# The dilated stage's first norm kept as one number per token, its row spread inside the second weight group

## The chip, the cores and the metric

The kernel runs on one core of one Trainium2 chip. The metric is the device time of one execution in microseconds (us); the median of several executions counts. TensorE (PE) multiplies matrices, VectorE (DVE) and ScalarE (ACT) work element by element, GpSimd (POOL) makes the low halves of the weights, and SyncE (SP) issues the weight transfers.

## The reference

Two transformer blocks follow one another on 512 tokens of width 1024. The second layer of the second block is the dilated attention. Its keys and values come from a norm of their own of the residual stream `x`:

```
def rmsnorm(x, g):
    xf = x.astype(jnp.float32)
    y = xf * lax.rsqrt(jnp.mean(xf * xf, axis=-1, keepdims=True) + RMS_EPS)
    return (y * g).astype(x.dtype)
...
    kv = (rmsnorm(x, kv_norm) @ w_kv).reshape(B, S, 2, N_GROUPS, ATT_HEADS, ATT_HEAD_DIM)
...
    h = rmsnorm(x, norm_mix_pre[layer])
    m = dilated_mixer(h, att_w_q[bi], att_w_o[bi], k_sh, v_sh, pos)
```

Both norms are of the same `x`, so they share one number per token, the reciprocal root of the mean square. It is this number, for all 512 tokens, that the change makes in another way.

## The kernel before

Everything is held with features on the 128 partitions and tokens along the row. `x` is eight tiles of 128 features by 512 tokens. A product of full precision is three matmuls of 512 columns (lines 702, 703 and 704: high by high, low by high, high by low); one such triple of one 128 by 128 weight tile is a k-step, and eight k-steps fill a bank. The gain of the norm is put into the operand (`h_hi` by ACT, `h_lo` by DVE), the reciprocal root is multiplied in later, when a bank is taken out (evicted).

The order on each engine is that of the code, with semaphores between engines. The start of the dilated stage (the function `dilated` of each engine) runs so:

1. The postnorm of the stage before updates `x` tile by tile. As each tile is ready ACT makes its high halves and its squares `SQD` (`dil_sq` in the trace), DVE the low halves.
2. PE runs the **first group**: three banks together, eight k-steps each, with the operands `H2H`, `H2L`.
3. PE adds up the squares with eight products of the 128 by 128 matrix of ones (the stationary operand) by `SQD[:, k, :]` (512 columns), line 1156. The result is a whole bank: on every partition the sum of each of 512 tokens. Each product shows in the trace as two matmuls.
4. PE runs the **second group**: two banks together, eight k-steps each, with `HH`, `HL` (`h_hi`, `h_lo`), each k waiting for its `h_lo` of line 2206. Four more banks follow singly.
5. DVE meanwhile: the fourth `h_lo`, then (`variance`, line 1613) mean and epsilon over 128x512; ACT takes the root of 128x512 (`std`, line 1206); DVE makes the fifth `h_lo`, then the reciprocal over 128x512 (`inverse`, line 1619) into `RSTD`, then the last three `h_lo`. It multiplies `RSTD` into the cosines and sines (line 2301), and evicts nine banks in the order `DIL_FIRST_OUT = (4, 0, 1, 2, 6, 3, 5, 7, 8)`. The first to be evicted is the second bank of the second group, and it waits until that group is done.
6. The first scores (`s_pair`, line 1053) wait until the rotary sums of six of these banks are done (`rotated`, line 2230).

Elsewhere in the kernel the same norm is made in columns: `column_sums` (line 733) takes 128 tokens of the squares as the stationary operand and one column of ones as the moving one, four products for 512 tokens, each again two matmuls in the trace; `spread` (line 742) turns a column of 128x4 numbers back into a row on all partitions by four transposes.

Of the kernel before, what the change touches and what calls it, by code (L numbers as in the profile page):

```python
# [20 lines left out]
ALU = mybir.AluOpType  # L21
ACT = mybir.ActivationFunctionType
# [4 lines left out]
D = 1024  # L27
KT = D // P
# [9 lines left out]
EPS = 1e-6  # L38
# [4 lines left out]
S0, TURN, OUTB = 3, 5, 7  # L43
# [97 lines left out]
DIL_FIRST_BANKS = (0, 1, 3, 4, 5, 6, 0, 1, 0)  # L141
# [142 lines left out]
def by_class(x):  # L284

    return x.rearrange("p (j r) -> p r j", r=4)


def in_class(x):

    return x.rearrange("p (r j) -> p r j", r=4)
# [12 lines left out]
def two_stacks_kernel(nc, d, out):  # L304
# [3 lines left out]
    with ExitStack() as ctx:  # L308
        sems = {n: ctx.enter_context(nc.semaphore(n)) for n in SEMAPHORES}

        def sb(name, shape, dt=F32):
            return ctx.enter_context(nc.sbuf_tensor(name, shape, dt))

        X = sb("x_res", [P, KT, SEQ])
        HH = sb("h_hi", [P, KT, SEQ], F32R)
        HL = sb("h_lo", [P, KT, SEQ], F32R)
# [6 lines left out]
        ONES = sb("ones", [P, P])  # L323
        RSTD = sb("rstd", [P, SEQ])
        RSTD2 = sb("rstd2", [P, SEQ])
        VAR = sb("var", [P, SEQ])
# [8 lines left out]
        def at(name, shape, offset, dt=F32):  # L335
            size = int(np.prod(shape[1:])) * 4
            assert offset + size <= arena_bytes, (name, offset + size, arena_bytes)
            return nc.alloc_sbuf_tensor_at(name, shape, dt, offset=base + offset)
# [82 lines left out]
        SQD = at("dil_sq", [P, KT, SEQ], 33 * T1)  # L421
# [12 lines left out]
        def sm(c, n=1):  # L434
            return SM[:, c:c + n]

        def gain(name, k=0):
            c = GAINS[name] + k
            return G[:, c:c + 1]

        banks = [ctx.enter_context(nc.psum_tensor(f"bank{b}", [P, SEQ], F32)) for b in range(8)]
# [201 lines left out]
        def _(pe):  # L643
            t = Tally(pe)

            class Programs:
                mine, stage = "stage_pe", 0
                n, tiles, rot, steps, gates = 0, 0, 0, 0, 0
# [60 lines left out]
                    for k in range(KT):  # L709
                        self.kt(bank, hi, lo, k, k == 0, k == KT - 1)  # L710

                def together(self, opened, hi, lo, nk, fresh, spread=None):

                    for k in range(nk):
                        if k == 1 and spread is not None:
                            self.spread(spread)
                        if k >= nk - fresh:
                            pe.wait_ge(sems["operand"], t.at("operand", k + 1 - nk))
                        elif k == 0:
                            pe.wait_ge(sems["operand"], t.at("operand", -fresh))  # L720
                        for bank in opened:
                            self.kt(bank, hi, lo, k, k == 0, k == nk - 1)
# [22 lines left out]
                def mix(self, l):  # L745
# [88 lines left out]
                    def turn(n, i):  # L834
                        _, blocks = key_blocks(KINDS[n], i)
                        if t.k.get("pt_copied", 0):
                            pe.wait_ge(sems["pt_copied"], t.at("pt_copied", CREDITS["pt_copied"]))
                        if i == 0:
                            pe.wait_ge(sems["v_token"], t.at("v_token"))
                        for m in range(group(KINDS[n])):  # L840
                            t.up("probs")
                            pe.wait_ge(sems["probs"], t.at("probs"))
                            for b in range(blocks):
                                ins = pe.transpose(banks[TURN + m][:, b * P:(b + 1) * P], SS[i % 2][m][:, b * P:(b + 1) * P], ID[:])  # L844
                            ins.then_inc(sems["turned"], t.one("turned"))
                            t.up("pt_copied")
# [178 lines left out]
                def dilated(self):  # L1025
# [125 lines left out]
                    opened = [self.open(b) for b in DIL_FIRST_BANKS[0:3]]  # L1151
                    self.together(opened, H2H, H2L, KT, KT)
                    for k in range(KT):
                        t.up("dil_squared")
                        pe.wait_ge(sems["dil_squared"], t.at("dil_squared"))
                        ins = pe.matmul(banks[OUTB][:], ONES[:], SQD[:, k, :], start=(k == 0), stop=(k == KT - 1))
                    ins.then_inc(sems["summed"], t.one("summed"))
                    t.up("operand", KT)
                    self.together([self.open(b) for b in DIL_FIRST_BANKS[3:5]], HH, HL, KT, KT)
                    base = self.tiles - 5  # L1160
                    out = {x: base + DIL_FIRST_OUT.index(at_) for at_, x in enumerate(DIL_FIRST)}
                    for at_ in range(5):
# [1 line left out]
                    for at_, x in list(enumerate(DIL_FIRST))[5:]:  # L1164
                        bank = self.open(DIL_FIRST_BANKS[at_])
# [18 lines left out]
        def _(act):  # L1184
            t = Tally(act)
# [12 lines left out]
            def root():  # L1198
                t.up("var_ready")
                act.wait_ge(sems["var_ready"], t.at("var_ready"))  # L1200
                act.activation(sm(INV, QT), sm(INV, QT), ACT.Sqrt).then_inc(sems["std_ready"], t.one("std_ready"))

            def std():
                t.up("var_ready")
                act.wait_ge(sems["var_ready"], t.at("var_ready"))
                act.activation(VAR[:], VAR[:], ACT.Sqrt).then_inc(sems["std_ready"], t.one("std_ready"))

            class Programs:
                mine, stage = "stage_act", 0
                n, tiles = 0, 0  # L1210
# [281 lines left out]
                def dilated(self):  # L1492
# [75 lines left out]
                            act.activation(in_class(HH[:, j, :]), by_class(X[:, j, :]), ACT.Copy, scale=gain("kv", j)).then_inc(sems["kv_hi"], t.one("kv_hi"))  # L1568
                    t.up("cleared", 6)
                    self.past(3, KT)  # L1570
                    std()
                    self.past(2, KT)
                    self.past(1, KT)
                    self.v_out(DVT[0][:, 0], DAUX)
# [16 lines left out]
        def _(dve):  # L1591
            t = Tally(dve)
# [13 lines left out]
                dve.tensor_tensor(lo, src, hi.bitcast(F32), ALU.subtract).then_inc(sems[name], t.one(name))  # L1606
                dve.wait_ge(sems[name], t.at(name))

            def variance(bank, n, placed=lambda x: x, taken=lambda x: x):

                t.up("summed")
                dve.wait_ge(sems["summed"], t.at("summed"))
                dve.tensor_scalar(placed(VAR[:]), taken(banks[bank][:]), 1.0 / n, EPS, ALU.mult, ALU.add).then_inc(sems["var_ready"], t.one("var_ready"))

            def inverse(dst=RSTD):

                t.up("std_ready")
                dve.wait_ge(sems["std_ready"], t.at("std_ready"))
                dve.reciprocal(dst[:], VAR[:]).then_inc(sems["dve_step"], t.one("dve_step"))
                dve.wait_ge(sems["dve_step"], t.at("dve_step"))  # L1620

            def rstd(bank, n, dst=RSTD):

                variance(bank, n)
                inverse(dst)

            def inverses(bank, n):

                t.up("summed")
                dve.wait_ge(sems["summed"], t.at("summed"))  # L1630
                dve.tensor_scalar(sm(INV, QT), banks[bank][:, 0:QT], 1.0 / n, EPS, ALU.mult, ALU.add).then_inc(sems["var_ready"], t.one("var_ready"))
                t.up("std_ready")
                dve.wait_ge(sems["std_ready"], t.at("std_ready"))
                dve.reciprocal(sm(INV, QT), sm(INV, QT)).then_inc(sems["inverted"], t.one("inverted"))

            def columns(bank):

                inverses(bank, D)
                t.up("rstd_spread")
                dve.wait_ge(sems["rstd_spread"], t.at("rstd_spread"))  # L1640
# [18 lines left out]
            class Programs:  # L1659
                mine, stage = "stage_dve", 0  # L1660
                n, tiles, steps = 0, 0, 0
# [539 lines left out]
                def dilated(self):  # L2201
                    self.postnorm(M2, (H2H, H2L, "mixpre1"), True)
                    for k in range(KT):
                        t.up("kv_hi")
                        dve.wait_ge(sems["kv_hi"], t.at("kv_hi"))
                        dve.scalar_tensor_tensor(in_class(HL[:, k, :]), by_class(X[:, k, :]), gain("kv", k),
                                                 in_class(HH[:, k, :].bitcast(F32)), ALU.mult, ALU.subtract).then_inc(sems["operand"], t.one("operand"))
                        if k == 3:
                            variance(OUTB, D, in_class, by_class)
                        elif k == 4:  # L2210
                            inverse()
                    t.up("dil_in", 96)
                    dve.wait_ge(sems["dil_in"], t.at("dil_in"))
                    t.up("cleared", 6)
# [88 lines left out]
                    n = self.n  # L2303
# [155 lines left out]
```

## Time and profile before

| | |
|---|---|
| median of 3 runs | 3001.33 us (2996.42 to 3001.58) |
| the profiled execution | 2998.37 us, of which the span is 2996.6 |
| PE busy | 2944.0 us, 98% |
| DVE busy | 1722.4 us, 57% |
| ACT busy | 1046.8 us, 35% |
| POOL busy | 1280.2 us, 43% |
| mean granted TensorE clock | 0.991 |

The span is the time from the first to the last instruction; 1.8 us lie around it. TensorE's clock has two levels, 1.2 and 2.4 GHz; the profile gives the granted clock as 0.50 and 1.00. The page's own chain of work is 94% PE.

### The profile page before, as it was taken

To read this page: it belongs to the slowest core of one execution; us is meant where nothing else is said; L and a number is where in the kernel's file an instruction comes from. 1 tells how busy PE (TensorE), PEld (TensorE's weight loads), DVE (VectorE), ACT (ScalarE), POOL (GpSimd) and SP (SyncE) were. 2 spreads that over 40 slices of the span, in tenths; PEclk is the share of its full clock that TensorE was granted. 3 is DMA by queue.
4 is the path that set the end of the run, shared out by engine and by line. 5 is a ranking of instruction groups with operands and counts; after the bars stand their busy time and mean duration, and the time that the engine had idled before them with its cause. 6 is when DMAs were issued, how large, how long until landed. Compare 5 with 4: busy or idle time off the path is not lost.

```text
span 2996.6 us, 38998 instructions
## 1 busy us (share of the span) xinstructions
PE 2944.0 (98%) x15208; PEld 2350.6 (78%) x15208; DVE 1722.4 (57%) x3008; ACT 1046.8 (35%) x1859; POOL 1280.2 (43%) x926
## 2 busy tenths in 40 slices
PE   8999999999999999999999999999999999999998
PEld 6777778877777778777778788887888888788886
DVE  4765455475745555735553587615766666587722
ACT  4443343354443432533322322224333333432221
POOL 3333334453333345544444455544434434355543
PEclk9999999999999999999999999999999999999999
DMA  5222222232222223232222233322222222223332
GB/s 192 83 78 66 71 79 96 85 112 71 78 64 71 78 85 99 85 106 78 85 85 79 83 99 97 98 94 94 79 78 72 78 78 78 71 87 97 99 99 70
DMA packets 78330, 260.21 MB, mean 87 GB/s; under 512 B 10730, under 2 KB 13546, under 8 KB 78148
## 3 DMA queue, kind: packets, MB, share of 16 engines
q1 hardware_dynamic: 77572, 255.63, 27.1%
q8 instruction: 121, 1.98, 0.3%
q10 hardware_dynamic: 576, 2.10, 0.2%
q14 instruction: 61, 0.50, 0.1%
HBM read 255.53 MB, written 6.09 MB: 87 GB/s over the span
## 4 chain that ended last, share of the span: by engine, by line
PE 94%; DVE 3%; DMA 1%; ACT 1%; issue 1%; POOL 0%; SPq 0%; DVEq 0%; ACTq 0%
PE bank L702 26%; PE bank L704 26%; PE bank L703 26%; PE bank L817 2%; PE bank L864 2%; PE bank L844 1%; PE bank L1017 1%; PE bank L970 1%; PE bank L972 1%; PE bank L971 1%; DVE x_res L1773 1%; PE bank L1053 1%; PE bank L733 1%; DMA bias_copies<-bias_vectors 1%; PE bank L1005 1%; PE bank L823 1%
## 5 line engine op out<-in xcount | busy, mean ns | idle before, releaser
L555 POOL TENSOR_TENSOR w_lo<-w_raw,w_hi 128x512 fp32r<-128x512 f32 x458 | 612.3, 1337 | 1633.1 <-ACT w_hi L1195 1633.1
L702 PE MATMUL bank<-h_hi,w_hi 128*128 128x512 f32 x2528 | 1012.8, 401 | 11.7 <-DVE h_lo L1761 6.6
L704 PE MATMUL bank<-h_hi,w_lo 128*128 128x512 f32 x2528 | 990.0, 392 | 0.0
L703 PE MATMUL bank<-h_lo,w_hi 128*128 128x512 f32 x2528 | 989.3, 391 | 0.0
L1195 ACT CAST w_hi<-w_raw 128x1024 fp32r<-128x1024 f32 x458 | 479.9, 1050 | 1263.2 <-PE bank L704 1185.4
L557 POOL TENSOR_TENSOR w_lo<-w_raw,w_hi 128x512 fp32r<-128x512 f32 x458 | 664.9, 1452 | 36.0
L702 PEld LDWEIGHTS bank<-h_hi,w_hi 128*128 128x128 f32 x2528 | 477.8, 189 | 118.0 <-issue 22.3
L704 PEld LDWEIGHTS bank<-h_hi,w_lo 128*128 128x128 f32 x2528 | 477.3, 189 | 103.2
L703 PEld LDWEIGHTS bank<-h_lo,w_hi 128*128 128x128 f32 x2528 | 478.2, 189 | 93.7 <-issue 0.6
L2042 DVE TENSOR_SCALAR m<-bank,gains 128x512 f32<-128x512 f32 x48 | 36.0, 751 | 328.6 <-ACT ta L1391 197.0
L1326 ACT ACTIVATE probs<-probs,small_columns 128x128 f32<-128x128 f32 (+2 forms) x192 | 101.9, 531 | 168.3 <-DVE small_columns L1820 164.1
L704 PE MATMUL bank<-f_hi,w_lo 128*128 128x512 f32 x352 | 137.0, 389 | 0.0
L703 PE MATMUL bank<-f_lo,w_hi 128*128 128x512 f32 x352 | 137.0, 389 | 0.0
L702 PE MATMUL bank<-f_hi,w_hi 128*128 128x512 f32 x352 | 136.9, 389 | 0.0
L1815 DVE CUSTOM_DVE_ANT_0 probs<-bank,bias 128x256 f32<-128x256 f32 (+3 forms) x128 | 56.4, 441 | 93.7 <-PE bank L817 90.1
L702 PE MATMUL bank<-zo_hi,w_hi 128*128 128x512 f32 x192 | 77.3, 403 | 0.0
L1336 ACT COPY pt<-bank 128x256 f32<-128x256 f32 (+3 forms) x160 | 55.4, 387 | 62.6 <-PE bank L844 62.5
L702 PEld LDWEIGHTS bank<-f_hi,w_hi 128*128 128x128 f32 x352 | 66.1, 188 | 13.8
L703 PEld LDWEIGHTS bank<-f_lo,w_hi 128*128 128x128 f32 x352 | 66.1, 188 | 13.7
L704 PEld LDWEIGHTS bank<-f_hi,w_lo 128*128 128x128 f32 x352 | 66.1, 188 | 13.7
L704 PE MATMUL bank<-zo_hi,w_lo 128*128 128x512 f32 x192 | 75.1, 391 | 0.0
L703 PE MATMUL bank<-zo_lo,w_hi 128*128 128x512 f32 x192 | 74.8, 390 | 0.0
(292 smaller groups left out, 4133.4 us busy)
## 6 DMA issues: line engine op xcount, KB each, us to landing
w_raw<-in_w SPq DMA_DIRECT2D x458, 512.0 KB, 3.5
bias_copies<-bias_vectors SPq DMA_DIRECT2D x1, 2560.0 KB
x_res<-in_x_t ACTq DMA_DIRECT2D x4, 512.0 KB, 8.5
bias<-bias_copies SPq DMA_DIRECT2D x8, 256.0 KB, 3.3
bias<-bias_copies SPq DMA_DIRECT2D x16, 128.0 KB, 2.4
out_x<-x_res SPq DMA_DIRECT2D x8, 256.0 KB, 2.0
bias_copies<-bias_vectors SPq DMA_DIRECT2D x1, 1280.0 KB
ple_raw<-in_p_t SPq DMA_DIRECT2D x2, 512.0 KB, 3.7
```

Source lines behind the costliest of these rows:

```text
L555: pool.tensor_tensor(WL[slot][:, 0:half], RAW[slot][:, 0:half], WH[slot][:, 0:half].bitcast(F32), ALU.subtract).then_inc(sems["lo_half"], 1)
L557: pool.tensor_tensor(WL[slot][:, half:], RAW[slot][:, half:], WH[slot][:, half:].bitcast(F32), ALU.subtract).then_inc(sems["lo_done"], 1)
L702: pe.matmul(banks[bank][:], WH[slot][:, w], hi[:, k, :], start=start, stop=False)
L703: pe.matmul(banks[bank][:], WH[slot][:, w], lo[:, k, :], start=False, stop=False)
L704: pe.matmul(banks[bank][:], WL[slot][:, w], hi[:, k, :], start=False, stop=stop).then_inc(sems["kt_done"], 1)
L817: ins = pe.matmul(banks[S0 + m][:, 0:blocks * P], AQ[r, q], keys[r, kk], start=True, stop=(kind != "mla"))
L864: ins = pe.matmul(banks[OUTB][r, i * P:(i + 1) * P], v, p[:, b * P:(b + 1) * P], start=(b == 0), stop=(b == blocks - 1))
L1195: act.copy(WH[slot][:], RAW[slot][:]).then_inc(sems["hi_done"], t.one("hi_done"))
L1326: act.activation(s, s, ACT.Exp, bias=sm(NM + u), accum_out=sm(DEN + u)).then_inc(sems["exped"], t.one("exped"))
L1336: act.copy(p[:, 0:w], banks[TURN + m][:, 0:w]).then_inc(sems["pt_copied"], t.one("pt_copied"))
L1815: dve.tensor_tensor_reduce(SS[i % 2][m][:, 0:w], banks[S0 + m][:, 0:w], bias, 1.0, LOWEST, ALU.add, ALU.max, sm(MX + u)).then_inc(sems["dv ...
L2042: dve.tensor_scalar(m[:, tile, :], bank[:], gain(f"{g}{l}", tile), None, ALU.mult).then_inc(sems[step], t.one(step))
```

## The change

The eight products by the ones matrix become 32 products of one column each, through `column_sums`, and their result is 128x4. Mean, root and reciprocal are then taken over 128x4. The row is spread by `spread` on PE, in front of the sixth k (k == 5) of the second group, and DVE copies it from the bank into `RSTD` after its last `h_lo`, with the rearrangement of tokens (`in_class`, `by_class`) that `variance` had done before.

```diff
-                def together(self, opened, hi, lo, nk, fresh, spread=None):
+                def together(self, opened, hi, lo, nk, fresh, spread=None, spread_at=1):
                     for k in range(nk):
-                        if k == 1 and spread is not None:
+                        if k == spread_at and spread is not None:
                             self.spread(spread)
...
                         pe.wait_ge(sems["dil_squared"], t.at("dil_squared"))
-                        ins = pe.matmul(banks[OUTB][:], ONES[:], SQD[:, k, :], start=(k == 0), stop=(k == KT - 1))
+                        ins = self.column_sums(OUTB, SQD[:, k, :], first=(k == 0), last=(k == KT - 1))
                     ins.then_inc(sems["summed"], t.one("summed"))
                     t.up("operand", KT)
-                    self.together([self.open(b) for b in DIL_FIRST_BANKS[3:5]], HH, HL, KT, KT)
+                    self.together([self.open(b) for b in DIL_FIRST_BANKS[3:5]], HH, HL, KT, KT, OUTB, 5)
...
-                    std()
+                    root()
...
                         if k == 3:
-                            variance(OUTB, D, in_class, by_class)
+                            squares_out(OUTB, D)
                         elif k == 4:
-                            inverse()
+                            inverses_out()
+                    t.up("rstd_spread")
+                    dve.wait_ge(sems["rstd_spread"], t.at("rstd_spread"))
+                    dve.tensor_scalar(in_class(RSTD[:]), by_class(banks[OUTB][:]), 1.0, None, ALU.mult).then_inc(sems["dve_step"], t.one("dve_step"))
+                    dve.wait_ge(sems["dve_step"], t.at("dve_step"))
```

The functions `squares_out` and `inverses_out` are the two halves of what `inverses` did before, over 128x4.

On PE, between the first and the second group and before the second group's sixth k, the order changes so (`bank<-ones,dil_sq` are the column sums, `bank<-ident,small_columns` the transposes of the spread):

```order
-L1156 MATMUL bank<-dil_sq,ones 128x512 [waits dil_squared] x8
+L733 MATMUL bank<-ones,dil_sq 128x1 [waits dil_squared]
+L733 MATMUL bank<-ones,dil_sq 128x1 x3
...
 L702 MATMUL bank<-h_hi,w_hi 128x512 [waits operand,lo_half,evicted]
 L703 MATMUL bank<-h_lo,w_hi 128x512
...
+L742 MATMUL bank<-ident,small_columns 128x128 [waits inverted]
+L742 MATMUL bank<-ident,small_columns 128x128 x3
 L702 MATMUL bank<-h_hi,w_hi 128x512 [waits operand]
```

Eight groups of four column products, one group per tile of squares, stand where eight wide ones stood, and four transposes have been put into the second group.

On DVE, at the same place of the stage, this stood before:

```order
L2206 SCALAR_TENSOR_TENSOR h_lo<-x_res,gains,h_hi 128x512 x4
L1613 TENSOR_SCALAR var<-bank 128x512
L2206 SCALAR_TENSOR_TENSOR h_lo<-x_res,gains,h_hi 128x512
L1619 RECIPROCAL rstd<-var 128x512
L2206 SCALAR_TENSOR_TENSOR h_lo<-x_res,gains,h_hi 128x512 x3
L2301 TENSOR_TENSOR tb<-tb,rstd 128x512
```

and now:

```order
L2191 SCALAR_TENSOR_TENSOR h_lo<-x_res,gains,h_hi 128x512 x4
L1608 TENSOR_SCALAR small_columns<-bank 128x4
L2191 SCALAR_TENSOR_TENSOR h_lo<-x_res,gains,h_hi 128x512
L1614 RECIPROCAL small_columns<-small_columns 128x4
L2191 SCALAR_TENSOR_TENSOR h_lo<-x_res,gains,h_hi 128x512 x3
L2199 TENSOR_SCALAR rstd<-bank 128x512
L2290 TENSOR_TENSOR tb<-tb,rstd 128x512
```

Two wide operations have become narrow ones in their places, and one wide copy has been added behind the last `h_lo`. On ACT one root of 128x512 has become one of 128x4, in its place.

## Rows read from the trace of the kernel before

**Rows 1.** Chain that ended last, 2030 to 2200 us: start us, us, what.

```profile
2073.04 6.88 PE bank L1156 x16
...
2081.97 3.34 DVE rstd L1619
```

**Rows 2.** Timeline of PE: start us, us, engine, line, operation, count, idle before.

```profile
2072.87 7.03 PE L1156 MATMUL bank<-dil_sq,ones 128*128 128x512 f32 x16
...
2079.97 0.40 PE L703 MATMUL bank<-h_lo,w_hi 128*128 128x512 f32 x1
...
2089.21 0.39 PE L704 MATMUL bank<-h_hi,w_lo 128*128 128x512 f32 x1
...
2089.87 0.40 PE L703 MATMUL bank<-h_lo,w_hi 128*128 128x512 f32 x1
...
2090.80 0.39 PE L704 MATMUL bank<-h_hi,w_lo 128*128 128x512 f32 x1
...
2114.26 0.49 PE L1053 MATMUL bank<-dil_k,dil_q 64*128 64x128 f32 x4 [0.36 <-DVE dil_k L2230]
```

**Rows 3.** Timeline of DVE at the same place.

```profile
2079.94 0.69 DVE L1613 TENSOR_SCALAR var<-bank 128x512 f32<-128x512 f32 x1 [6.82 <-PE bank L1156]
...
2089.40 1.73 DVE L2301 TENSOR_TENSOR tb<-tb,rstd 128x512 f32<-128x512 f32 x1
...
2091.77 0.69 DVE L2234 TENSOR_TENSOR rstd<-bank,rstd 128x512 f32<-128x512 f32 x1
```

**Rows 4.** Timeline of PE in the next stage, column sums and a spread.

```profile
2643.54 0.95 PE L733 MATMUL bank<-ones,sq 128*128 128x1 f32 x8
...
2644.67 0.40 PE L703 MATMUL bank<-h_lo,w_hi 128*128 128x512 f32 x1
...
2646.99 0.39 PE L704 MATMUL bank<-h_hi,w_lo 128*128 128x512 f32 x1
...
2647.88 0.39 PE L703 MATMUL bank<-h_lo,w_hi 128*128 128x512 f32 x1
```

**Rows 5.** Timeline of PE in the first block: 24 column sums in a row, twice.

```profile
116.75 0.95 PE L733 MATMUL bank<-ones,da_sq 128*128 128x1 f32 x8
117.55 1.93 PE L733 MATMUL bank<-ones,lat_sq 128*128 128x1 f32 x16
119.34 0.62 PE L702 MATMUL bank<-h_hi,w_hi 128*128 128x512 f32 x1
...
741.60 0.95 PE L733 MATMUL bank<-ones,da_sq 128*128 128x1 f32 x8
```

**Rows 6.** A reciprocal over 128x4 (DVE timeline).

```profile
2048.68 0.18 DVE L1634 RECIPROCAL small_columns<-small_columns 128x4 f32<-128x4 f32 x1 [0.35 <-ACT small_columns L1201]
```

**Rows 7.** The copy of a spread row, by its line: duration min/median/max in ns.

```profile
L1645 DVE COPY rstd<-bank x5: 691/692/692, 37.5 to 2647.8; 128x512 f32<-128x512 f32 x5
```

**Rows 8.** Stretches: from:to, length, PE busy, granted clock, DMA share, GB/s.

```profile
119.50:120.00 0.50, 0.50 (x2) 0.52 0.00 0
...
122.50:123.00 0.50, 0.50 (x3) 0.57 0.75 303
...
744.00:744.50 0.50, 0.50 (x5) 0.66 0.00 0
```

**Rows 9.** Last column sums of the first post stage, PE timeline in narrow windows.

```profile
583.94 0.56 PE L733 MATMUL bank<-ones,tb 128*128 128x1 f32 x2
...
584.15 0.35 PE L733 MATMUL bank<-ones,tb 128*128 128x1 f32 x1
```

**Rows 10.** PE timeline behind them, to the return of the clock.

```profile
584.97 0.77 PE L702 MATMUL bank<-ple_hi,w_hi 128*128 128x512 f32 x1 [0.47 <-ACTq L1219]
...
590.62 0.39 PE L704 MATMUL bank<-ple_hi,w_lo 128*128 128x512 f32 x1
```

**Rows 11.** PE timeline at the end of the retention stage's products.

```profile
1674.27 0.40 PE L704 MATMUL bank<-ret_hi,w_lo 128*128 128x512 f32 x1
```

**Rows 12.** Stretch behind it: length, busy of five engines, clock, DMA share, GB/s.

```profile
1678.00:1680.00 2.00, 0.62 (x4) 0.41 (x4) 1.10 (x3) 0.03 (x1) 0.49 (x1) 0.85 0.19 41
```

More of the change, by code:

```diff
@@ L1201, in root @@
                 act.activation(sm(INV, QT), sm(INV, QT), ACT.Sqrt).then_inc(sems["std_ready"], t.one("std_ready"))
[L1203 to L1206, printed above, removed]
             class Programs:
@@ L1607, in split, with squares_out @@
                 dve.wait_ge(sems[name], t.at(name))
[L1609 to L1627, printed above, removed]
+            def squares_out(bank, n):
                 t.up("summed")
@@ L1631, in inverses, with inverses_out @@
                 dve.tensor_scalar(sm(INV, QT), banks[bank][:, 0:QT], 1.0 / n, EPS, ALU.mult, ALU.add).then_inc(sems["var_ready"], t.one("var_ready"))
+            def inverses_out():
                 t.up("std_ready")
@@ L1634, in inverses @@
                 dve.reciprocal(sm(INV, QT), sm(INV, QT)).then_inc(sems["inverted"], t.one("inverted"))
+            def inverses(bank, n):
+                squares_out(bank, n)
+                inverses_out()
             def columns(bank):
@@ L2208, in dilated @@
                         if k == 3:
-                            variance(OUTB, D, in_class, by_class)
+                            squares_out(OUTB, D)
                         elif k == 4:
-                            inverse()
+                            inverses_out()
+                    t.up("rstd_spread")
+                    dve.wait_ge(sems["rstd_spread"], t.at("rstd_spread"))
+                    dve.tensor_scalar(in_class(RSTD[:]), by_class(banks[OUTB][:]), 1.0, None, ALU.mult).then_inc(sems["dve_step"], t.one("dve_step"))
+                    dve.wait_ge(sems["dve_step"], t.at("dve_step"))
                     t.up("dil_in", 96)
```

## The prediction

> **What bounds the kernel now.** I read the page first (PE is busy 98% of the span), then the chain that ended last around the change, then the timelines of PE and DVE there, and last the granted clock over the whole span in steps of 2 us, with steps of 0.5 us where it fell.
>
> The chain shows the reader one place where PE is not the bound. It goes through the sums of squares (6.88 us), then leaves PE for DVE, takes the wide reciprocal (3.34 us) on the way [rows 1], and returns to PE only at the first scores, at 2114.26, which had waited for a rotated key [rows 2]. PE idled 0.36 us there. Matmuls of 0.39 us follow one another every 0.227 us, so without the wait the scores would have started 0.16 us before the modelled end as well: PE could have been there 0.52 us earlier. This is all that any saving on DVE can bring in this stage, because from 2115 to 2600 us PE waits for nobody.
>
> What DVE does between the sums and that wait is one unbroken row of work: mean at 2079.94, sines and cosines from 2089.40, first eviction at 2091.77 [rows 3]. But the first eviction is of the second group's second bank, whose last matmul starts at 2090.80 and ends at 2091.19 [rows 2]. DVE is there only 0.58 us after PE. If DVE comes earlier by more than that, it waits for PE.
>
> **The change part by part, at the full clock.**
>
> *The sums.* Before: from the first wide matmul at 2072.87 to the second matmul of the next group at 2079.97 it is 7.10 us [rows 2]. After: a set of eight narrow matmuls in the same surroundings takes from 2643.54 to 2644.67, 1.13 us to the same point [rows 4]; the change has 64 of them. The step between them is (1.93 - 0.25) / 15 = 0.112 us within the 16 of [rows 5], where 0.25 is one narrow matmul. So 1.13 + 56 x 0.112 = 7.40 us: +0.30 on PE. That one column moves in place of 512 brings nothing: each of the 64 loads its own 128 by 128 weights, and that sets the step. The sum is ready for DVE 0.95 + 56 x 0.112 = 7.22 us after the start, at 2080.09 and not at 2079.94: +0.15.
>
> *The spread.* A triple's third matmul at 2646.99, four transposes, and the second matmul of the next triple at 2647.88: 0.89 us, where two steps of 0.227 would be 0.45 [rows 4]: +0.44 on PE. The wait for `inverted` in front of it costs nothing: even the wide reciprocal began 2.03 us after the mean (2079.94 to 2081.97 [rows 1, 3]), the narrow one takes 0.18 [rows 6], and k == 5 starts 10 k-steps of 0.68, 6.8 us, after them.
>
> *The late low halves.* DVE makes the last three `h_lo` behind the reciprocal, and PE waited for the last of them: from 2089.21 to 2089.87 it is 0.66 us in place of 0.45 [rows 2]. These 0.21 us go, as the narrow reciprocal saves 3.33 - 0.18 = 3.15 us in front of them. PE in all: +0.30 + 0.44 - 0.21 = +0.53.
>
> *DVE.* The multiplication of cosines began 9.46 us after the mean (2079.94 to 2089.40). Now the row is in the bank about 7.2 us after the sum (6.8 and four transposes), later than the last `h_lo`; the copy takes 0.69 [rows 7], as the wide mean with the same rearrangement did [rows 3]. That is 8.0 us, so DVE gains about 1.4, less 0.15. Of this only 0.58 us could count before DVE waits for the second group, and that group itself now ends 0.53 later. So the first eviction moves by 0.53 - 0.58 = -0.05, and the 22.5 us of evictions after it move with it. PE is at the scores at 2113.74 + 0.53 = 2114.27. Both are where they were: **0.0 us at the full clock**. ACT's narrower root (0.4 us less) lies beside PE's work and is worth nothing.
>
> **The clock.** This is the term that decides. In the first block 24 narrow matmuls stand in a row, from 116.75 to 119.34 [rows 5]. PE is busy all the time, and still the granted clock falls from 1.00 to 0.50 at about 119.5, and is back at about 122.9 [rows 8]: 2.7 us after the sums began, for 3.4 us. The same happens behind the same 24 in the second layer (sums from 741.60 [rows 5], fall at 744.2 [rows 8], 2.6 us after). Nothing else makes the clock fall while PE is busy. It also falls in each of the stages' ends, where 8 and 8 narrow matmuls stand with waits between. After the change 64 stand in a row for 7 us, so I take it to fall here, where the wide sums held it at 1.00.
>
> The Trainium skill ("TensorE: Matmul & The Clock Gate", the table on why this matters) gives another rule: the clock drops because of idle gaps between bursts, and is kept by keeping the engine busy. By it nothing would fall here, as there is no gap, and the sum would stay 0.0; by the rows of the first block it falls. I follow the rows and keep the rule as a rival.
>
> *When it falls.* 2.6 us after the start of the sums at the earliest seen. The latest fall after the last wide matmul that I find is behind 1674.27 [rows 11]: the mean clock 0.85 in 1678 to 1680 [rows 12] puts it at 1679.4, 5.1 us. I take the middle, 3.8 us. Then (7.07 - 3.8) / 0.112 = 29 narrow matmuls are left (7.07 being the time to the next group's start). At 0.50 they stand 0.21 us apart (583.94 and 584.15 [rows 9]), 0.10 more each: +2.9 us. Bounds: 2.6 us leaves 40, +4.0; 5.1 us leaves 18, +1.8.
>
> *How long it stays.* Wide matmuls at 0.50 stand 0.427 us apart in place of 0.227, so 47% of the cold time is lost. The cold stretch of dense work lasted 3.4 us behind [rows 5], and from 584.97 to about 590.5, 5.5 us, at the longest [rows 10]. Middle 4.5: +2.1 us. Bounds +1.6 and +2.6. DVE's chain moves with PE by as much, since its first eviction waits for the second group, so nothing of it is hidden.
>
> Sum: 0.0 + 2.9 + 2.1 = **+5.0 us**, between +3.4 and +6.6.
>
> **The base.** The sum is made on the profiled execution, 2998.37 us, and gives 3003.4. The median of the three runs is 3.0 above it; the mean of all four is 2999.4. I set the base between that and the median, 3000.4, and forecast 3005.4. Single runs of this kernel lie 5 us apart, so 0.2% (6 us) is about what a measurement can tell from no change.
>
> **Rivals.**
>
> *The clock holds.* For it: the skill's rule above, and the wide sums at 1.00. Against it: the two falls in busy stretches less than half as long. Time +-0.3, 3000.4. Chance 0.10.
>
> *The clock stays down past the spread* (the slower side). The four transposes break the dense stretch, as they do behind [rows 10], the longest cold stretch. If the clock came back only after them, the ten k-steps before would run cold, 30 x 0.427 = 12.8 us, and 3.4 more behind: 0.47 x 16.2 = 7.6 in place of 2.1, in all +10.5, 3011. Against it: the ten k-steps are 6.8 to 12.8 us of dense work, longer than any cold stretch I find. It decides from a cold stretch of (6.0 - 2.9) / 0.47 = 6.6 us on. Chance 0.04.
>
> *DVE's gain shows* (the faster side). If the first eviction did not wait for the second group and PE's additions were hidden, the 0.52 us of waiting would go and the clock would have to hold too: 2999.9. Nothing speaks for it. Chance 0.02, and even then it is inside 0.2%.
>
> The likeliest, 0.84, is the fall with its cost of 3.4 to 6.6. It passes 6.0 only with an early fall and a late return, or by the scatter of the medians: I give that 0.16.
>
> **Numbers.** Slower by over 0.2%: 0.16 + 0.04 = 0.20. Faster: 0.02, for scatter alone. Within: 0.78. The range takes 3.4 and 6.6 with 2 to 2.5 us of scatter of the base: 3001 to 3009.
>
> **What the changed profile would show.** 64 narrow matmuls with dil_sq, 0.112 us apart and then 0.21, about 10 us in all; a granted clock of 0.50 from some 2.6 to 5 us after their start until 3.4 to 5.5 us into the second group; four transposes in its sixth k with no wait for `inverted`; DVE waiting about 1 us for the second group before its first eviction; the scores' wait for DVE at most some tenths. If the clock row stays at 1.00, the forecast is wrong by the whole 5 us. If the narrow matmuls stood closer than 0.112, the sums would be a gain.

## The result

The changed kernel takes 3003.74 us (median of 20 runs, 3000.54 to 3007.20), the kernel before 2998.18 us (20 runs, 2995.02 to 3002.76): **5.6 us slower, ratio 1.0019, 95% interval 1.0013 to 1.0025**. The profiled execution of the changed kernel has a span of 3003.0 us. The forecast was 5.0 us more and 3005.4 us. The kernel before has come out 3 us lower over 20 runs than over its first three.

Single executions of one kernel lie up to 8 us apart, as the ranges above show, so the profiles are compared by one stretch, from the first product of the dilated stage to the first scores. Before it is 2054.78 to 2114.26, 59.48 us. After it is 66.00 us, 6.52 more. Of the kernel before, the first product of the stage (PE's timeline), and the stretch of the wide sums up to the second group's start (length, busy of five engines, clock, DMA share, GB/s, as in [rows 12]), with the clock at 1.00:

```profile
2054.78 0.76 PE L702 MATMUL bank<-h_hi,w_hi 128*128 128x512 f32 x1 [4.70 <-DVE h_lo L1756]
2072.87:2079.34 6.47, 6.47 (x18) 2.88 (x16) 0.26 (x1) 4.00 (x4) 3.30 (x3) 1.00 0.52 187
```

PE's timeline of the changed kernel, answering to [rows 2]:

```profile
2054.59 0.77 PE L702 MATMUL bank<-h_hi,w_hi 128*128 128x512 f32 x1 [4.67 <-DVE h_lo L1741]
...
2072.62 11.39 PE L733 MATMUL bank<-ones,dil_sq 128*128 128x1 f32 x64
...
2083.87 0.77 PE L702 MATMUL bank<-h_hi,w_hi 128*128 128x512 f32 x1
2084.45 0.63 PE L703 MATMUL bank<-h_lo,w_hi 128*128 128x512 f32 x1
...
2088.71 0.41 PE L704 MATMUL bank<-h_hi,w_lo 128*128 128x512 f32 x1
2088.97 0.40 PE L702 MATMUL bank<-h_hi,w_hi 128*128 128x512 f32 x1
...
2093.07 0.60 PE L742 MATMUL bank<-ident,small_columns 128*128 128x128 f32 x4
...
2120.59 0.49 PE L1053 MATMUL bank<-dil_k,dil_q 64*128 64x128 f32 x4
```

The sums take 11.25 us, to 2083.87, where the wide ones took 6.47. Behind them the wide matmuls take 0.63 us each and stand 0.43 apart, until 2088.7. The granted clock of the same execution says why (stretches as in [rows 8]):

```profile
2074.00:2075.00 1.00, 1.00 (x12) 1.00 1.02 414
2075.00:2076.00 1.00, 1.00 (x8) 0.54 0.70 287
...
2083.00:2084.00 1.00, 1.00 (x6) 0.50 0.85 328
2088.00:2089.00 1.00, 1.00 (x5) 0.63 0.00 0
2089.00:2090.00 1.00, 1.00 (x6) 1.00 0.00 0
```

PE is busy in every one of these microseconds. The clock goes from 2.4 to 1.2 GHz at 2075.08, 2.5 us after the sums began (0.08 us at full speed and 0.92 at half give the mean of 0.54 in that microsecond). It is back at 2088.74, 4.9 us into the second group. Last, DVE, answering to [rows 3]:

```profile
2084.05 0.16 DVE L1608 TENSOR_SCALAR small_columns<-bank 128x4 f32<-128x4 f32 x1 [11.18 <-PE bank L733]
...
2093.70 0.69 DVE L2199 TENSOR_SCALAR rstd<-bank 128x512 f32<-128x512 f32 x1 [5.20 <-PE bank L742]
...
2097.88 0.69 DVE L2223 TENSOR_TENSOR rstd<-bank,rstd 128x512 f32<-128x512 f32 x1 [1.06 <-PE bank L704]
```

DVE's part of the norm is short, and what it gained it waits away: 5.20 us for the transposes and 1.06 us for the second group.

### The profile page after: what moved, and what is told of

The parts are those of the page before. It is cut to its first block, busy times and chain, and to the rows that moved or that the text cites. A ratio compares the mean times of both kernels' runs of the same rounds, so it can differ in the third digit from the quotient of the medians.

```text
span 3003.0 us, 39102 instructions
## 1 busy us (share of the span) xinstructions
PE 2950.8 (98%) x15260; PEld 2361.2 (79%) x15260; DVE 1718.4 (57%) x3009; ACT 1046.3 (35%) x1859; POOL 1277.7 (43%) x926
## 4 chain that ended last, share of the span: by engine, by line
PE 95%; DVE 2%; DMA 1%; ACT 1%; issue 0%; POOL 0%; SPq 0%; PEldq 0%; DVEq 0%; ACTq 0%; PEld 0%
PE bank L702 27%; PE bank L704 26%; PE bank L703 26%; PE bank L817 2%; PE bank L864 2%; PE bank L844 1%; PE bank L1017 1%; PE bank L970 1%; PE bank L733 1%; PE bank L972 1%; PE bank L971 1%; DVE x_res L1758 1%; PE bank L1053 1%; DMA bias_copies<-bias_vectors 1%; PE bank L1005 1%; PE bank L823 1%
```

## The experiments

Each ratio is to the kernel before, run beside it; for the experiments both ran on the same chip. The ratio is not the quotient of the two medians, so the two can differ: e8's medians lie 3.1 us apart, its ratio stands for 4.8. The stretch is read from the profiled execution as above, one for each kernel.

| run | ratio (95%) | median, its before | stretch, us |
|---|---|---|---|
| kernel before | 1 | | 59.48 |
| the change | 1.0019 (1.0013 to 1.0025) | 3003.74, 2998.18 | 66.00 |
| e1_cols128 | 0.9990 (0.9981 to 0.9999) | 2997.23, 2998.14 | 59.50 |
| e2_inter | 0.9997 (0.9989 to 1.0006) | 2998.01, 2998.14 | 60.01 |
| e3_spread3 | 1.0019 (1.0010 to 1.0028) | 3004.93, 2998.14 | 66.03 |
| e4_dvesum | 1.0003 (0.9994 to 1.0011) | 2999.44, 2998.14 | 60.93 |
| e5_early | 1.0002 (0.9993 to 1.0011) | 2998.12, 2998.47 | 59.35 |
| e6_dve_early | 1.0008 (0.9999 to 1.0017) | 3000.25, 2998.47 | 61.54 |
| e7_pool_early | 0.9997 (0.9988 to 1.0006) | 2997.06, 2998.47 | 58.51 |
| e8_round_early | 0.9984 (0.9975 to 0.9993) | 2995.04, 2998.16 | 56.85 |
| e9_round | 0.9998 (0.9989 to 1.0007) | 2997.44, 2998.16 | 58.85 |

### e1_cols128: the same products, 128 columns each

```diff
-                        ins = self.column_sums(OUTB, SQD[:, k, :], first=(k == 0), last=(k == KT - 1))
+                        for b in range(QT):
+                            ins = pe.matmul(banks[OUTB][:, b * P:(b + 1) * P], SQD[:, k, b * P:(b + 1) * P], ONES[:],
+                                            start=(k == 0 and b == 0), stop=(k == KT - 1 and b == QT - 1), skip_group_check=True)
...
-                dve.tensor_scalar(sm(INV, QT), banks[bank][:, 0:QT], 1.0 / n, EPS, ALU.mult, ALU.add).then_inc(sems["var_ready"], t.one("var_ready"))
+                dve.tensor_scalar(sm(INV, QT), banks[bank][:, 0:QT * step:step], 1.0 / n, EPS, ALU.mult, ALU.add).then_inc(sems["var_ready"], t.one("var_ready"))
```

> The change with one thing altered: each of the 64 products of the sums moves 128 columns of ones in place of one (same number of products, same weight loads, same place, same spread; the result stands four times 128 columns wide and its first columns are read). Theory (the clock falls because only one column moves per product): the granted clock stays 1.00 through the sums, the products stand 0.11 to 0.12 us apart, the sums take 7.1 to 7.5 us in place of 11.25, the second group starts warm, and the time is 0 to 0.5 us above the kernel before, about 5.5 below the change. Rival (the 64 weight loads, or so many short products, are what costs): the sums still take 10 us or more and the time is that of the change, 5 to 6 us above the kernel before.

PE's timeline, and two stretches within the sums (as in [rows 12]):

```profile
2071.89 7.30 PE L1157 MATMUL bank<-ones,dil_sq 128*128 128x128 f32 x64
2078.95 0.48 PE L702 MATMUL bank<-h_hi,w_hi 128*128 128x512 f32 x1
2079.26 0.40 PE L703 MATMUL bank<-h_lo,w_hi 128*128 128x512 f32 x1
...
2113.38 0.49 PE L1053 MATMUL bank<-dil_k,dil_q 64*128 64x128 f32 x4
```

```profile
2074.00:2076.00 2.00, 2.00 (x20) 2.00 (x19) 0.00 (x0) 1.05 (x1) 0.17 (x1) 1.00 0.78 320
2076.00:2078.00 2.00, 2.00 (x20) 2.00 (x19) 0.00 (x0) 1.82 (x2) 1.92 (x2) 1.00 0.09 35
```

The 64 products stand 0.112 us apart to the end, and the clock is 1.00 in every stretch from 2070 to 2095. From their start to the second matmul of the next group it is 7.37 us, where the prediction had 7.40 for narrow ones at the full clock. The stretch is that of the kernel before, and the interval of the ratio lies wholly below that of the change. The same number of products with the same weight loads in the same place thus costs nothing when each moves 128 columns, and 6.5 us when each moves one. The 5.6 us are the clock's, and the narrow column is its cause. The rival that the loads themselves cost is out. Only 1 and 128 columns were run; what lies between them is not shown.

### e2_inter: eight narrow products behind each k of the first group

```diff
-                    self.together(opened, H2H, H2L, KT, KT)
                     for k in range(KT):
+                        pe.wait_ge(sems["operand"], t.at("operand", k + 1 - KT))
+                        for bank in opened:
+                            self.kt(bank, H2H, H2L, k, k == 0, k == KT - 1)
                         t.up("dil_squared")
                         pe.wait_ge(sems["dil_squared"], t.at("dil_squared"))
-                        ins = self.column_sums(OUTB, SQD[:, k, :], first=(k == 0), last=(k == KT - 1))
+                        ins = self.column_sums(DAUX, SQD[:, k, :], first=(k == 0), last=(k == KT - 1))
...
-                            squares_out(OUTB, D)
+                            squares_out(DAUX, D)
```

> The change with the narrow products moved: the eight of each tile of squares stand behind the same k of the first group (into a bank of their own) and not all 64 behind the group. The number and form of the products are the same. Theory (64 narrow ones in a row let the clock fall): the clock stays 1.00 from 2059 us on, the first group is longer by about 7.2 us, the second starts where it started before, and the time is within 0.5 us of the kernel before. Rival (narrow products cost by themselves, wherever they are): some 5 us above the kernel before. Rival (breaking the dense group lets the clock fall in several places): more than 6 us above.

PE's timeline, the first two and the last of the eight sets, and two stretches (as in [rows 8]):

```profile
2060.79 0.95 PE L733 MATMUL bank<-ones,dil_sq 128*128 128x1 f32 x8
2063.77 0.95 PE L733 MATMUL bank<-ones,dil_sq 128*128 128x1 f32 x8
...
2081.61 0.95 PE L733 MATMUL bank<-ones,dil_sq 128*128 128x1 f32 x8
```

```profile
2061.00:2062.00 1.00, 1.00 (x9) 1.00 0.06 16
...
2079.00:2080.00 1.00, 1.00 (x9) 1.00 0.16 66
```

Every set takes what the eight of [rows 4] take, the clock is 1.00 from 2061 us on, and the stretch is 0.53 us longer than before. So one column per product is harmless when 2 us of wide products stand between each eight. From one set to the next it is 2.98 us, of which the nine wide matmuls between take 9 x 0.227 = 2.04; a set thus costs 0.94 us, and eight cost 7.5. The prediction's 7.40 for the 64 in a row holds one wide matmul as well; without it (0.23) it is 7.2.

### e3_spread3: the spread two k earlier

```diff
-                    self.together([self.open(b) for b in DIL_FIRST_BANKS[3:5]], HH, HL, KT, KT, OUTB, 5)
+                    self.together([self.open(b) for b in DIL_FIRST_BANKS[3:5]], HH, HL, KT, KT, OUTB, 3)
```

> The change with the row spread in front of the fourth k of the second group and not of the sixth. Theory (the transposes cost PE 0.44 us wherever they are, and DVE is held by the second group's end): DVE copies the row 1.4 us or more earlier and then waits that much longer for the group; the time is that of the change within 0.3 us. Rival (DVE's multiplications are on the path): 1 us or more below the change. Rival (the column is not ready at the fourth k): a wait of PE for it, and a time above the change.

DVE's timeline, and the clock (as in [rows 8]):

```profile
2079.41 0.16 DVE L1608 TENSOR_SCALAR small_columns<-bank 128x4 f32<-128x4 f32 x1 [11.11 <-PE bank L733]
...
2086.41 0.69 DVE L2199 TENSOR_SCALAR rstd<-bank 128x512 f32<-128x512 f32 x1 [2.56 <-PE bank L742]
...
2093.31 0.69 DVE L2223 TENSOR_TENSOR rstd<-bank,rstd 128x512 f32<-128x512 f32 x1 [4.88 <-PE bank L704]
```

```profile
2070.00:2071.00 1.00, 1.00 (x10) 0.82 0.97 397
...
2084.00:2085.00 1.00, 1.00 (x5) 0.85 0.00 0
```

DVE copies the row 7.0 us after the mean in place of 9.65, and waits 4.88 us for the second group in place of 1.06. The stretch is that of the change within 0.03 us and so is the ratio. A faster norm on DVE is worth nothing here: the first eviction waits for the group. In this execution the sums began at 2068.07; the clock fell at 2070.64, 2.6 us later, and came back at 2084.3. The execution took 3000.28 us and the change's profiled one 3004.82, with the same stretch, so these 4.5 us lie elsewhere in the kernel.

### e4_dvesum: the squares added on DVE

```diff
+                        for j in {3: (1, 2, 3), 4: (4, 5), 5: (6, 7)}.get(k, ()):
...
+                            dve.tensor_tensor(SQD[:, 0, :], SQD[:, 0, :], SQD[:, j, :], ALU.add).then_inc(sems[name], t.one(name))
```

> The squares are added over the eight tiles on DVE (seven additions of 128x512 of 0.7 us, among the low halves of the second group), so PE has 8 narrow products and not 64, in front of the fifth k of the second group; the spread stands in front of the eighth. PE thus loses 6.5 us of sums of the kernel before. Theory A (the second group's weights are the next thing to be late: in the kernel before GpSimd finished the first low half for it only at about 2077.4, and PE started at 2079.3): PE starts the group some 2 us earlier and not 6.5, then waits for weights, and the time is 1 to 2 us below the kernel before. Theory B (the sums are all on the path): 5 to 6 us below the kernel before. Theory C (DVE, with 5 us more of work, becomes the bound): within 0.5 us of the kernel before or above it. The clock may fall in the wait for the weights; that would add 1.6 to 2.6 us.

PE's timeline and stretches (as in [rows 8]):

```profile
2077.10 0.76 PE L702 MATMUL bank<-h_hi,w_hi 128*128 128x512 f32 x1 [4.36 <-POOL w_lo L555]
...
2115.26 0.49 PE L1055 MATMUL bank<-dil_k,dil_q 64*128 64x128 f32 x4 [0.55 <-DVE dil_k L2224]
```

```profile
2076.00:2078.00 2.00, 0.90 (x2) 0.50 0.05 20
2078.00:2080.00 2.00, 2.00 (x6) 0.50 0.21 23
```

With the sums gone PE stood 4.4 us, waiting for the low halves of the second group's first weights, and the clock fell in the wait. So theory A held in its mechanism: behind the sums stood another wait, which they had covered. The group started 22.8 us after the stage's first product (2054.33), where it started 24.6 us after it in the kernel before (2079.34): the weights had been ready only about 1.8 us early. The 1 to 2 us that theory A forecast did not come; with the cold stretch after the wait the stretch is 1.45 us longer than before. By its number the result is theory C's (the ratio cannot be told from 1), but its mechanism is not shown: DVE, additions and all, stood waiting 2.55 us for the transposes. These stand late, in front of the eighth k, and so the first eviction starts 0.7 us behind the group's end.

### e5_early: the weights early, all else as before

```diff
-            load(FIRST["dil"] + RING)
+            load(FIRST["dil"] + 2 * RING)
...
             lows(FIRST["dil"] + RING)
+            lows(FIRST["dil"] + RING + 2)
...
+                        if k == KT - 1:
+                            hi(self.n + 2 * KT)
```

> The kernel before, with wide sums, and the weights of the second group made ready earlier: their transfers are issued before the stage's tables, ACT makes two chunks' high halves in front of its last five operands, GpSimd makes their low halves before it clears the probabilities. Theory (the wide sums, 6.5 us, hid the lateness of these weights, of which the first low half was ready at 2077.4 against a start at 2079.3): nothing changes, within 0.5 us of the kernel before from the stage's first product to the first scores. Rival (the order of transfers matters by itself): 1 us or more either way.

The stretch is 59.35 us against 59.48: the order of transfers is worth nothing while wide sums cover it. The weights were in fact earlier: GpSimd began their first low half 14.4 us after the stage's first product (2070.69 and 2056.27), where it was 21.2 us before (2075.96 and 2054.78).

### e6_dve_early: DVE's additions with the weights early

The edit is that of e4 and e5 together, with the narrow products in front of the seventh k.

> The squares added on DVE and 8 narrow products on PE, as in the run before, now with the weights of the second group ready early. Theory (the 4.4 us of waiting for the low half, with the clock's fall in it, ate the gain): PE starts the second group right behind the first, the clock stays 1.00, and then DVE's extra 5 us of additions bound the stage: the stretch from the stage's first product to the first scores is 3 to 5 us shorter than in the kernel before, and so is the time. Rival (the gain was not there at all): within 0.5 us of the kernel before.

DVE's timeline, one row of GpSimd's and PE's two waits:

```profile
2069.79 7.09 DVE L2194 SCALAR_TENSOR_TENSOR h_lo<-x_res,gains,h_hi 128x512 fp32r<-128x512 f32 x4
2076.80 3.19 DVE L2201 TENSOR_TENSOR dil_sq<-dil_sq 128x512 f32<-128x512 f32 x3
```

```profile
2070.14 1.91 POOL L555 TENSOR_TENSOR w_lo<-w_raw,w_hi 128x512 fp32r<-128x512 f32 x1 [20.45 <-ACT w_hi L1196]
```

```profile
2081.22 0.50 PE L703 MATMUL bank<-h_hi,w_hi 128*128 128x512 f32 x1 [1.76 <-DVE h_lo L2194]
...
2085.49 0.51 PE L703 MATMUL bank<-h_hi,w_hi 128*128 128x512 f32 x1 [2.60 <-DVE h_lo L2194]
```

A miss: 2.06 us longer than before. The four low halves that took 4.32 us in one row of the kernel before (1.08 each) take 7.09 here, 1.77 each, while GpSimd makes the weights beside them, whose own operations take 1.9 us in place of 1.3. PE went from the first group into the second without a gap, so the time of the sums was gained there. It was lost again in two waits for low halves of the operand, 1.76 and 2.60 us, and the clock fell at about 2086.6. DVE's additions stand in front of these halves, and the halves before them took 2.8 us longer; how much of the loss is whose, no run separates. The longer halves alone did no harm: in e5 the same four take 7.19 us, and DVE then waits 3.95 us for the wide sums.

### e7_pool_early: the squares added on GpSimd

```diff
+            for k in range(1, KT):
+                pool.wait_ge(sems["dil_squared"], k + 1)
...
+                pool.tensor_tensor(SQD[:, 0, :], SQD[:, 0, :], SQD[:, k, :], ALU.add).then_inc(sems["pool_added"], 1)
```

> As the run with early weights, but the squares are added on GpSimd, which stands idle from 2050 to 2066 us, while the first group runs; PE has 8 narrow products right behind the first group, and the row is spread in front of the fourth k of the second. Theory: PE loses 6.5 of the 7.1 us of sums, gains 0.44 for the spread, and DVE is held by the second group's end alone: 5.5 to 6.3 us shorter than the kernel before in the stage and in the time, ratio 0.998. Rival (GpSimd's additions slow DVE, which shares operands with it while it updates x tile by tile, and so the first group): 3 us or less.

DVE's, GpSimd's and PE's timelines:

```profile
2054.94 1.74 DVE L1763 TENSOR_TENSOR x_res<-x_res,m 128x512 f32<-128x512 f32 x1
```

```profile
2054.71 1.42 POOL L565 TENSOR_TENSOR dil_sq<-dil_sq 128x512 f32<-128x512 f32 x1 [0.57 <-ACT dil_sq L1564]
```

```profile
2071.22 0.95 PE L739 MATMUL bank<-ones,dil_sq 128*128 128x1 f32 x8
2078.02 0.65 PE L748 MATMUL bank<-ident,small_columns 128*128 128x128 f32 x4 [1.50 <-DVE small_columns L1619]
```

The rival won. While GpSimd added, DVE's additions to x took up to 1.74 us in place of 0.69, the first group took 21.4 us (2049.81 to 2071.22) in place of 18.1, and the spread in front of the fourth k came 1.5 us too early for its column, as the four low halves in front of the mean took 7.97 us in place of 4.32. Of 6 us hoped for 1.0 is left in the stretch, and the ratio cannot be told from 1.

### e8_round_early and e9_round: one matmul per wide product

```diff
+        ONESR = sb("ones_r", [P, P], F32R)
...
-        SQD = at("dil_sq", [P, KT, SEQ], 33 * T1)
+        SQD = at("dil_sq", [P, KT, SEQ], 33 * T1, F32R)
...
-                        ins = pe.matmul(banks[OUTB][:], ONES[:], SQD[:, k, :], start=(k == 0), stop=(k == KT - 1))
+                        ins = pe.matmul(banks[OUTB][:], ONESR[:], SQD[:, k, :], start=(k == 0), stop=(k == KT - 1))
```

Both keep the norm of the kernel before, wide on every engine; e8 has the early weights as well.

> The kernel before with its wide sums, but the squares and the ones in the rounded 32-bit form that the weight products use, so that each of the eight products is one matmul of 0.227 us and not two of 0.43 (the squares are rounded before they are added); and the weights of the second group ready early. Theory: PE loses 16 x 0.43 - 8 x 0.227 = 5.1 us of sums, nothing is added to DVE or GpSimd, the clock stays 1.00, and the wide norm on DVE is still done when the second group is: the stretch to the first scores is 4 to 5 us shorter than in the kernel before, the ratio 0.9985. Rival (DVE, with the wide reciprocal in front of its last low halves, becomes late for the second group): 2 to 3 us shorter. Rival (as in the runs with fewer products, something else takes the gain): within 1 us.

> The same rounded wide sums without the early weights. Theory (the second group's first low half is ready 22.6 us after the stage's first product, as in the kernel before and in the run with 4.4 us of waiting for it): PE waits for it 2.5 to 3 us behind the sums, the group starts 1.9 us earlier than before, and the stretch is 1 to 2 us shorter than in the kernel before, or about equal if the clock falls in the wait. Rival (the weights are no limit): as the run with early weights.

PE's timeline of e8_round_early:

```profile
2074.49 2.02 PE L1158 MATMUL bank<-dil_sq,ones_r 128*128 128x512 f32 x8
...
2084.42 0.50 PE L704 MATMUL bank<-h_hi,w_hi 128*128 128x512 f32 x1 [1.11 <-DVE h_lo L2212]
...
2113.27 0.49 PE L1055 MATMUL bank<-dil_k,dil_q 64*128 64x128 f32 x4 [0.55 <-DVE dil_k L2236]
```

and of e9_round:

```profile
2081.56 0.47 PE L703 MATMUL bank<-h_hi,w_hi 128*128 128x512 f32 x1 [3.00 <-POOL w_lo L556]
```

e8 beats both kernels: 3.1 us below the kernel before in the median, ratio 0.9984 with an interval below 1, and 2.63 us in the stretch. It is no equal exchange, since the squares are rounded before they are added; what that does to the result was not measured. The eight products take 1.85 us to the next group's start and not 6.47. Of these 4.6 us, 1.7 go to waits for the last low halves (the rival named for it: the wide reciprocal stands in front of them; and the three take 5.51 us beside GpSimd's work, 4.15 before), and of the remaining 2.9 the stretch shows 2.63. Without the early weights, e9, PE waits 3.00 us for them, the clock falls at 2082.6, and 0.63 us are left in the stretch; the ratio cannot be told from 1.

## Why the prediction was right

The forecast was 5.0 us more, by the fall of the clock; measured were 5.6 in the medians. Step by step, against the changed kernel's profiled execution, whose stretch grew by 6.52 us:

- **The clock falls in the 64 products although PE is busy.** The granted clock of the changed kernel shows the fall, and e1 its cause: there the products differ in the number of moving columns alone, and nothing falls. The Trainium skill's rule of idle gaps ("TensorE: Matmul & The Clock Gate", the table on why this matters) does not cover this case: there was no gap, and the clock fell.
- **When it falls: 3.8 us after the sums' start, bounds 2.6 to 5.1.** Measured 2.5 here and 2.6 in e3, at or just below the early bound, so the sums lost more: to the second group's start they run 11.25 us in place of 7.07, +4.2 where the forecast had +2.9 and at most +4.0. This is the term that was mis-sized, and its middle was a choice: the two falls of the first block, with PE busy, came 2.6 and 2.7 us after the sums' start, while the late bound of 5.1 came from a stretch in which PE was busy for only 0.62 of 2 us [rows 12]. The cold step of 0.21 us was right: the last four start within 0.64 us (2083.02, 0.99 us for four of 0.35).
- **How long it stays: 4.5 us of the second group, +2.1.** Measured 4.9 us, which at 47% is +2.3.
- **The sums at the full clock, +0.30, and the spread, +0.44.** e1 shows 7.37 us for 7.40, and from 2085.62 to 2086.51 around its spread, 0.89 us, as worked out.
- **The late low halves, -0.21, and the wait for the column, nothing.** No matmul of the changed kernel waits for a low half or for `inverted` in the second group, and none of e1, at the full clock.
- **DVE's gain is worth nothing because the first eviction waits for the second group.** The forecast was a wait of about 1 us; it is 1.06, and 0.89 in e1 at the full clock. e3 adds 3.8 us to that wait and nothing to the time.
- **Sum at the full clock, 0.0.** e1's stretch is +0.02.

The sum for the profiled execution would be 0.0 + 4.2 + 2.3 = 6.5, against 6.52 measured. The change's medians differ by 1.0 us less than that, but e3's, with the same stretch, by 6.8 us. The difference may be scatter, or the fall may come later in some executions; two profiles do not settle it.

Two errors of opposite sign stand in the forecast time: the base of 3000.4 was 2.2 us above the median of 20 runs and the change 0.6 us below the measured one, so 3005.4 lies 1.7 us above 3003.74. Against the stretch the 5.0 us were 1.5 too few, close to the upper bound of 6.6.

What the prediction did not see is the wait behind the sums. It read only that the second group started with its weights ready, and e4 showed that they were ready only about 1.8 us before. This did not touch the forecast, since the sums became longer and not shorter. A change that really shortened them would have been misjudged: e8 and e9, which differ in these weights alone, are 2.0 us apart in the stretch.

## What to carry to other kernels

Before many tiny products are put in a row, look at the granted clock where the same kernel already has some: PE's busy share does not show the price. Here products with one moving column cost as much time as ones with 128 (e1), and both ways of avoiding the clock's fall took nearly all of the loss away: widening them (e1, stretch +0.02 us) and setting them between wide ones, eight at a time (e2, +0.53). And when work is taken off the bounding engine, ask what was ready just in time behind it: here it was the weights, and with rounded sums the gain was 0.63 us of the stretch as they were and 2.63 when they were moved too.

## What was not expected of the hardware

- Narrow and wider products have the same step: 0.112 us apart both with 1 and with 128 moving columns (64 in 7.06 us in e1), and 0.213 us with 1 column at the lower clock.
- The wide products of plain 32-bit operands show as two matmuls 0.43 us apart, those of rounded operands as one of 0.23: 6.47 us against 1.85 for the same eight sums.
- GpSimd's additions over 128x512 beside DVE's: DVE's operation of 0.69 us took 1.74 in places, and the first group became 3.3 us longer. The kernel before has such a row too, 1.73 us [rows 3], while GpSimd makes a low half of the weights. It is the time side by side that is shown, and not the reason.
